# A hybrid recurrence-and-attention block: each projection of the attention stage in two halves of k, with score units and maxima between them

## What is computed

```python
h = rmsnorm(x, norm_w)
z = h @ w_in
hq, hf, hi, hg, aqkv, ag, gates = jnp.split(z, IN_SPLITS, axis=-1)
...
q_b = apply_rope(aqkv[:, :, 0], cos, sin)
k_b = apply_rope(aqkv[:, :, 1], cos, sin)
v_b = aqkv[:, :, 2]
for g, (window, dilation) in enumerate(ATT_GROUPS):
    o_g, m_g, l_g = dilated_window_attention(q_b[:, :, g], k_b[:, :, g], v_b[:, :, g], window, dilation)
...
wts = jnp.exp(ms - jnp.max(ms, axis=0))
den = jnp.sum(wts * jnp.stack(dens), axis=0)
num = jnp.sum(wts[..., None] * jnp.stack(outs), axis=0)
o_b = (num / den[..., None]).reshape(B, S, ATT_DIM) * jax.nn.silu(ag)
```

## Time and profile before

| | |
|---|---|
| median of 3 runs | 1621.53 us (1619.78 to 1624.89) |
| profiled execution: time, span | 1620.52 us, 1618.7 us |
| mean granted TensorE clock | 0.992 |
| TensorE matmuls busy | 1577.8 us (97% of the span) |
| vector engine busy | 823.7 us (51%) |
| scalar engine busy | 671.5 us (41%) |
| GpSimd busy | 110.4 us (7%) |

### The profile page before, as it was taken

How to read it: one execution, slowest core, us unless ns; L and a number is a source line. 1 busy time by engine, 2 the same in 40 slices (tenths; PEclk the granted TensorE clock), 3 DMA queues, 4 the chain that set the end, 5 groups by cost and what they waited for, 6 DMA issues and landing times. The chain is left out here.

```text
span 1618.7 us, 22138 instructions
## 1 busy us (share of the span) xinstructions
PE 1577.8 (97%) x8628; PEld 1331.0 (82%) x8628; DVE 823.7 (51%) x1242; ACT 671.5 (41%) x826; POOL 110.4 (7%) x66
## 2 busy tenths in 40 slices
PE   4999999999999999999999999999999999999998
PEld 4788888888888888888888887888788878878897
DVE  6854536363636454453751575257524764644423
ACT  5645556463636465554322333232333234411311
POOL 3940000000000000001300000000000000000000
PEclk9999999999999999999999999999999999999999
DMA  5111111111111111112311212111211113233511
GB/s 205 40 40 53 66 52 56 47 52 65 52 52 52 65 52 39 52 65 65 105 53 53 53 53 66 55 53 53 66 53 53 53 59 119 85 137 124 218 56 79
DMA packets 33900, 113.80 MB, mean 70 GB/s; under 512 B 5339, under 2 KB 5789, under 8 KB 33821
## 3 DMA queue, kind: packets, MB, share of 16 engines
q1 hardware_dynamic: 33828, 112.82, 21.6%
HBM read 81.77 MB, written 18.45 MB: 62 GB/s over the span
## 5 line engine op out<-in xcount | busy, mean ns | idle before, releaser
L638 PE MATMUL z_ps<-h_hi,w_hi 128*128 128x512 f32 x1392 | 559.8, 402 | 0.0
L640 PE MATMUL z_ps<-h_hi,w_lo 128*128 128x512 f32 x1392 | 551.5, 396 | 0.0
L639 PE MATMUL z_ps<-h_lo,w_hi 128*128 128x512 f32 x1392 | 551.1, 396 | 0.0
L640 PEld LDWEIGHTS z_ps<-h_hi,w_lo 128*128 128x128 f32 x1392 | 263.1, 189 | 62.0
L638 PEld LDWEIGHTS z_ps<-h_hi,w_hi 128*128 128x128 f32 x1392 | 263.6, 189 | 57.7 <-issue 0.4
L639 PEld LDWEIGHTS z_ps<-h_lo,w_hi 128*128 128x128 f32 x1392 | 263.6, 189 | 56.8
L1224 DVE TENSOR_TENSOR w_lo<-w_stage,w_hi 128x1024 fp32r<-128x1024 f32 x87 | 108.5, 1248 | 313.5 <-ACT w_hi L971 313.5
L979 ACT ACTIVATE zz<-z_ps 128x512 f32<-128x512 f32 x48 | 28.7, 598 | 214.2 <-PE z_ps L640 143.0
L979 ACT ACT_TABLE_LOAD x61 | 78.3, 1283 | 87.1 <-PE z_ps L640 86.3
L971 ACT ACTIVATE w_hi<-w_stage 128x1024 fp32r<-128x1024 f32 x89 | 93.6, 1051 | 0.4
L806 PE MATMUL pc<-pt,vb 128*128 128x128 f32 x560 | 76.9, 278 | 0.7 <-ACT pt L1129 0.7
(11 more groups left out here) (250 smaller groups left out, 2363.7 us busy)
## 6 DMA issues: line engine op xcount, KB each, us to landing
w_stage<-w_in SPq DMA_DIRECT2D x88, 512.0 KB, 3.5
z_swap<-zz SPq DMA_DIRECT2D x96, 128.0 KB, 2.3
gate_d<-gate SPq DMA_DIRECT2D x16, 512.0 KB, 3.8
x_in<-x SPq DMA_DIRECT2D x8, 512.0 KB, 7.1
o_a_d<-o_a SPq DMA_DIRECT2D x8, 512.0 KB, 4.9
w_stage<-w_a SPq DMA_DIRECT2D x8, 512.0 KB, 3.4
cos_t<-gate_d SPq DMA_DIRECT2D x8, 512.0 KB, 3.3
sin_t<-gate_d SPq DMA_DIRECT2D x8, 512.0 KB, 4.3
```

Source lines behind the costliest of these rows:

```text
L638: nc.tensor.matmul(z_ps[hf][:], w_hi[s][:, k, :], h_hi[:, k, t], start=k == 0, stop=False)
L639: nc.tensor.matmul(z_ps[hf][:], w_hi[s][:, k, :], h_lo[:, k, t], start=False, stop=False)
L640: last = nc.tensor.matmul(z_ps[hf][:], w_lo[s][:, k, :], h_hi[:, k, t], start=False, stop=k == KT - 1)
```

## The change

`project` takes a range of k. In a pass that projects, TensorE now runs the front half of the projection (k = 0 to 3, 12 matmuls), then the slot's score units but the last and the first half of its maxima (the first head; in slot 16 both heads of (2, 0)), then the back half (k = 4 to 7), then the last unit and the other maxima. The waits for the weights and for the bank stay at the front half, the increment of `z_made` at the back half. The scalar engine computes the exponentials of all units but the last ahead of its copies and of the evacuation, that of the last behind them, as before. In the last pass (i = 4, no projection) the order is the old one. The vector engine, GpSimd and SP are unchanged, and no instruction is added or left out.

```diff
+            front, back = range(0, KT // 2), range(KT // 2, KT)
+
+            def project(n, s, hf, ks=range(KT)):
+
+                if ks[0] == 0:
+                    if hf == 0:
+                        pe.wait_ge(w_lo_done, n + 1)
+                    pe.wait_ge(z_taken[hf], n)
                 t = slice(HALF * hf, HALF * (hf + 1))
-                for k in range(KT):
+                for k in ks:
...
-                last.then_inc(z_made[hf], 1)
+                if ks[-1] == KT - 1:
+                    last.then_inc(z_made[hf], 1)
...
             def attention(i, prev, cur):
                 for slot in range(2 * AT_CHUNKS):
                     c = slot // 2
+                    units = UNIT_SLOTS.get(slot, ()) if prev else ()
+                    peaks = [(g, m, h) for g, m in MAX_SLOTS.get(slot, ()) for h in range(2)] if cur else []
+
+                    def unit(u):
+                        scores_t(i, u)
+                        if u:
+                            weighted(i, u - 1)
+
                     if cur:
-                        project(N_HG + i * AT_CHUNKS + c, c % 2, slot % 2)
+                        project(N_HG + i * AT_CHUNKS + c, c % 2, slot % 2, front)
+                        for u in units[:-1]:
+                            unit(u)
+                        for g, m, h in peaks[:len(peaks) // 2]:
+                            maxima(i, g, m, h)
+                        project(N_HG + i * AT_CHUNKS + c, c % 2, slot % 2, back)
...
                     if prev:
-                        for u in UNIT_SLOTS.get(slot, ()):
-                            scores_t(i, u)
-                            if u:
-                                weighted(i, u - 1)
+                        for u in units[-1:] if cur else units:
+                            unit(u)
...
-                    if cur:
-                        for g, m in MAX_SLOTS.get(slot, ()):
-                            for h in range(2):
-                                maxima(i, g, m, h)
+                    for g, m, h in peaks[len(peaks) // 2:]:
+                        maxima(i, g, m, h)
```

On the scalar engine, where `weigh(u)` is the old exponential with its waits:

```diff
+                    units = UNIT_SLOTS.get(slot, ()) if prev else ()
...
                     if cur:
+                        for u in units[:-1]:
+                            weigh(u)
                         if c < 6:
...
-                    if prev:
-                        for u in UNIT_SLOTS.get(slot, ()):
...
+                    for u in units[-1:] if cur else units:
+                        weigh(u)
```

More of the change, by code:

```diff
@@ L1096, in attention, with weigh @@
                             nc.scalar.activation(dst, pb[:, b, :].rearrange("p (c x e) -> p c x e", c=4, x=2), ACT.Copy).then_inc(av_taken, 1)
+                    units = UNIT_SLOTS.get(slot, ()) if prev else ()
+                    def weigh(u):
+                        act.wait_ge(st_made, (i - 1) * N_UNITS + u + 1)
+                        cols = sum(P * k for _, _, k in unit_keys(UNITS[u][0], UNITS[u][2]))
+                        if u >= 2:
+                            act.wait_ge(pu_made, (i - 1) * N_UNITS + u - 1)
+                        nc.scalar.activation(pt[u % 2][:, 0:cols], pb[:, u % 2, 0:cols], ACT.Exp).then_inc(pt_done, 1)
                     if cur:
+                        for u in units[:-1]:
+                            weigh(u)
                         if c < 6:
```

## The result

The changed kernel takes 1632.82 us (median of 4 runs, 1632.30 to 1633.10); the kernel before, run beside it, takes 1622.61 (4 runs, 1619.78 to 1624.89). The ratio is 1.0063, with a 95% interval from 1.0046 to 1.0081: slower by 0.6%. The forecast was 1633, slower. The experiments were timed in two later sessions, with 19 executions of the kernel before in one (median 1620.68) and 9 in the other (1620.62); one of the 19 took 1944.14 us at a granted clock of 0.754, and the ratios leave it out.

What follows compares the result with a forecast made beforehand. The prediction took TensorE, 97% busy, as the bound, so only its waits, clock and instruction stream count. Its terms, 7.6 + 1.5 + 2.8 + 0.7 = 12.6 us on 1620.5, gave 1633 us; stated range 1625 to 1641.

Steps and rivals of the forecast that it cites:

- What bounds the kernel: TensorE, 97% busy: only its own waits, clock and instruction stream move the end; one wait counts, maxima for row maxima, 8.2 us.
- The stop, +7.6: Slot 15, passes 1 to 3: first-head maxima ask earlier for row maxima released at an unchanged time, 2.52 us more each.
- The clock, +1.5: TensorE's granted clock falls after the slot 15 wait in all three passes, 1.53 us each, against 3.06 paid before.
- The breaks, +2.8: TensorE's stream changes kind more often: 31 projection halves starting behind f32 matmuls, 0.09 us each.
- The first pass, +0.7: Pass i = 0, without score units: early maxima wait for row maxima, 0.47 us in slot 13 and 0.24 in slot 15.
- The exponentials, 0: Scalar engine's exponentials moved ahead of the evacuation: worth nothing, since TensorE is never idle in those slots.
- (b): Rival, chance 0.07: slot 14's first-head row maxima are taken before k_full, the slot 15 waits vanish: -9.3 us, 1611.
- (a): Rival, chance 0.15: the slot 15 wait grows, the clock stays low for long (6.0 us), most breaks cost: +19.2, 1640.
- (c): Rival, chance 0.13: nothing measurable; low ends together, 1625, or the wait as long as now with only breaks added, 1623.

Runs made afterwards that it cites:

- the score units alone: Kernel before with only the score units and their exponentials moved between the projection halves, all maxima behind the back half: 1621.98 us, ratio to before 1.0008.
- without slot 15's early maxima: Changed kernel, but in slot 15 both heads' maxima stand behind the back half: 1622.55 us, ratio to before 1.0012.
- k = 6: Changed kernel with the projection divided at 6 instead of 4, so 18 matmuls ahead of the first head's maxima: 1626.71 us, ratio to before 1.0035.
- the maxima alone: Changed kernel with score units and exponentials back in the old place, only the early maxima between the halves: 1633.4 us, ratio to before 1.0076.
- slot 15 alone: Kernel before with only slot 15's first-head maxima moved between the projection halves: 1632.7 us, ratio to before 1.0076.
- k = 2: Changed kernel with the projection divided at 2 instead of 4, so 6 matmuls ahead of the first head's maxima: 1646.38 us, ratio to before 1.0155.

## Why the prediction was right, step by step

**What bounds the kernel.** Right. TensorE's list of waits held one entry that could move, and the move made it longer.

**The stop, +7.6.** Right in its mechanism (same release, earlier request). The waits were forecast at about 5.5 us each, 16 in all, and are 5.63 each, 17.2 in all with the small one. A pass without a fall of the clock was 19.40 before; with 2.52 added it would be 21.92. The passes took 23.65, 24.10 and 24.33; what is over, 1.7, 2.2 and 2.4, falls to the clock, if the 2.52 are right. The granted clock gives a check that does not assume them. It is low until 996.06, 1163.32 and 1330.57, and the stops end at 992.28, 1158.56 and 1325.29: 3.8, 4.8 and 5.3 us of low clock lie under work, 13.8 in all. The kernel before paid 1.53 for 3.41 us under work; at that rate these cost 6.2 (an estimate), 3.1 more than its two falls, and 10.8 - 3.1 = 7.7 are left for the stop. Slot 16 was to start 13.7 us behind the denominators' exponential; it started 15.2 behind it (982.13 to 997.35), the difference again being the clock's.

**The clock, +1.5: too small.** Three falls came, as forecast, but each was priced at the old 1.53. The granted clock of the three stretches is 0.86 (0.92 before): some 6.8 us at half speed in each against 3.4. The falls cost 6.3 us in all, against 3.1 in the kernel before: +3.2. It lies between the value taken and the upper end of +6.0, since part of the low stretch passes inside the stop (3.0 of the 6.8 us in the first pass). The row that came nearer was the start-up wait of the earlier trace rows, with its long low stretch; a longer stop was priced with the falls of a shorter one. By the Trainium skill's rule ("TensorE: Matmul & The Clock Gate", Terms) a fall of 6.8 us would cost half of it, 3.4, as an estimate; the passes show 1.7 to 2.4, for the same reason.

**The breaks, +2.8: too large.** The slots between, with nine moved score units and the early maxima of slots 8 to 13, cost 0.13 us a pass, 0.4 in all. The earlier trace rows were read from one side only. The first step of a projection behind `weighted()` is indeed 0.32, but then the last f32 matmuls of `weighted()` are shorter. In the changed kernel, behind 6 of them:

```profile
1051.87 0.83 PE L810 MATMUL pc<-pt,vb 128*128 128x128 f32 x6
1052.45 0.48 PE L641 MATMUL z_ps<-h_hi,w_hi 128*128 128x512 f32 x1
1052.77 0.40 PE L642 MATMUL z_ps<-h_lo,w_hi 128*128 128x512 f32 x1
```

and in the kernel before, in the same slot, 6 of them with the next score unit behind:

```profile
1051.93 0.83 PE L806 MATMUL pc<-pt,vb 128*128 128x128 f32 x6
1052.59 0.38 PE L774 MATMUL pb<-mask_b,ident_b 128*128 128x512 bf16 x1
```

The six take 0.58 us up to a projection and 0.66 up to a unit: 0.08 less, against the 0.09 more behind them. These are the rows of one place; the sum over all breaks is what the 0.4 us say. A start-to-start distance on one side of a border is no cost of the border; both sides have to be taken.

**The first pass, +0.7.** Right: +0.8. In slot 13 the early maxima start at 814.48 instead of 813.98, 0.50 us late where 0.47 was forecast (the list of waits, which counts from the modelled end of the matmul before, has 0.33 of it); in slot 15 they start 0.23 late, forecast 0.24, too short to stand in the list.

**The exponentials, 0.** Right: the one wait of `weighted()` is the old 0.7.

The sum, 12.6, met the difference of the two profiled executions, 12.6, but that it met it so closely is luck: two of its terms were off by +2.4 and -1.7, the stop and the first pass by a tenth or so, and head and tail, of which the prediction had nothing, gave +0.6. By medians the difference is 10.2 us with one session's runs of before, and 12.1 with the 19 runs of another (1620.68). The high end of the sum is 1642, and the range stated in the prediction ends at 1641; nothing hangs on that.

**The rivals.** (b), the stops vanish, fell with the vector engine's order, as was argued; the same gain was real, though, and came from the scalar engine's order. (a) was right that the clock stays low for longer, but put 6.0 us on it where 3.2 came, and had the breaks wrong. (c) did not occur.

## What to carry to other kernels

A wait whose release is at a fixed time, set by another engine's chain, cannot be shortened by asking earlier: here every microsecond of work that was moved from ahead of the request to behind it was added to the stop. So look first at what releases a wait, and whether it depends on anything that the change moves. Ask also whether the engine is idle between the parts that are to be interleaved: here it was not, and there was nothing to gain. When an engine waits, follow its releaser two or three engines back: here two neighbouring pieces of work on the scalar engine, in the other order, were worth 0.9% where the interleaving lost 0.6%.

## What was not expected of the hardware

How long the clock stays low does not follow the length of the stop evenly. The granted clock of the profiled executions, in passes 1, 2 and 3 of each kernel:

| stop, us | kernels | time at half clock, us |
|---|---|---|
| 2.7 | before | 3.4, 3.4, none |
| 2.7 | the score units alone | 3.4, 3.4, 3.4 |
| 2.9 to 3.0 | without slot 15's early maxima | none, 3.4, 3.4 |
| 4.2 | k = 6 | 6.8, 3.4, 6.8 |
| 5.4 to 5.6 | the change, the maxima alone, slot 15 alone | 6.8 nine times of nine |
| 7.0 | k = 2 | 10.2, 10.2, 10.2 |

What a low stretch costs depends on how much of it lies under work: 3.4 us under work cost 1.5, and 3.8, 4.8 and 5.3 us under work cost 1.7, 2.2 and 2.4. So the same stop does not always cost the same. Over the 16.07 us of a pass without a stop it was 3.3 us without a fall and 4.9 with one in the kernel before, and 7.6 to 8.3 in the changed one.
